# The delta layer's causal convolutions: one pass per tap over a whole channel group in place of three thirds

## The reference

```python
def causal_dwconv(u, buf, w):
    ext = jnp.concatenate([buf.astype(u.dtype), u], axis=1)
    y = ext[:, 0:t] * w[0]
    for j in range(1, CONV_W):           # CONV_W = 4
        y = y + ext[:, j:j + t] * w[j]
    return y, ext[:, t:]

def odd_layer(...):
    u = jnp.dot(hmod, w_in)
    qkv, z, b, a = jnp.split(u, ODD_SPLITS, axis=-1)
    qkv_c, new_buf = causal_dwconv(qkv, conv_buf, conv_w)
    qkv_c = jax.nn.silu(qkv_c).astype(jnp.float32)
    q, k, v = jnp.split(qkv_c, (GDN_KW, 2 * GDN_KW), axis=-1)
    ...                                  # 8 heads of 128: l2_normalize, gated_delta_rule, norm, gate, w_out
```

## Time and profile before

| | |
|---|---|
| time, median of 3 runs | 1657.87 us (1655.21 to 1658.93) |
| the profiled execution's own time | 1660.12 us |
| its span | 1658.3 us |
| PE busy | 1518.7 us, 92% of the span |
| DVE busy | 736.2 us, 44% |
| ACT busy | 410.8 us, 25% |
| POOL busy | 198.1 us, 12% |

### The profile page before, as it was taken

How to read it: one execution, slowest core, us unless ns; L and a number is a source line. 1 busy time by engine, 2 the same in 40 slices (tenths; PEclk the granted TensorE clock), 3 DMA queues, 4 the chain that set the end, 5 groups by cost and what they waited for, 6 DMA issues and landing times.

```text
span 1658.3 us, 32834 instructions
## 1 busy us (share of the span) xinstructions
PE 1518.7 (92%) x14320; PEld 934.1 (56%) x14320; DVE 736.2 (44%) x1650; ACT 410.8 (25%) x1036; POOL 198.1 (12%) x400
## 2 busy tenths in 40 slices
PE   4997999788869997898999999999999999999997
PEld 3554555455544445356766667666676766666533
DVE  4202455333331225264473654736557365562251
ACT  4001343333320004311231312313122131221220
POOL 1000000000001011002030120301213012020020
PEclk8898999999989996898999999999999999999999
DMA  8501111000051304011011110111111111030041
GB/s 336 215 13 44 42 32 62 1 1 1 3 224 58 145 0 170 8 42 42 28 53 31 39 43 29 54 30 39 43 40 43 42 43 27 15 138 3 30 150 64
DMA packets 53012, 100.52 MB, mean 61 GB/s; under 512 B 34458, under 2 KB 37346, under 8 KB 50290
## 3 DMA queue, kind: packets, MB, share of 16 engines
q1 hardware_dynamic: 52868, 98.41, 17.5%
HBM read 83.54 MB, written 14.86 MB: 59 GB/s over the span
## 4 chain that ended last, share of the span: by engine, by line
PE 55%; DVE 4%; issue 2%; ACT 1%; POOL 0%; POOLq 0%; DVEq 0%; ACTq 0%
PE psum L727 53%; PE psum L730 2%; DVE mem L1640 1%; DVE mem L2108 0%; DVE mem L2046 0%; DVE mem L1923 0%; DVE mem L1892 0%; DVE mem L1818 0%; ACT mem L1390 0%; DVE mem L1810 0%; DVE mem L2163 0%; DVE mem L1812 0%; DVE mem L1909 0%; ACT mem L1415 0%; ACT mem L1417 0%
## 5 line engine op out<-in xcount | busy, mean ns | idle before, releaser
L727 PE MATMUL psum<-mem 32*32 32x32 f32 (+9 forms) x13728 | 1441.1, 288 | 74.1 <-issue 23.8
L727 PEld LDWEIGHTS psum<-mem 32*32 32x32 f32 (+5 forms) x13728 | 859.9, 136 | 624.8 <-issue 286.2
L730 PE MATMUL psum<-mem 128*128 128x128 f32 (+1 forms) x592 | 97.1, 303 | 57.2 <-ACT mem L1275 14.2
L1892 DVE SCALAR_TENSOR_TENSOR mem<-mem 128x384 f32<-128x384 f32 (+1 forms) x216 | 138.0, 639 | 2.4
L730 PEld LDWEIGHTS psum<-mem 128*128 128x128 f32 (+1 forms) x592 | 76.7, 160 | 90.2 <-issue 61.9
L1810 DVE SCALAR_TENSOR_TENSOR mem<-psum,mem 128x512 f32<-128x512 f32 x13 | 9.8, 751 | 154.9 <-POOL mem L602 154.9
L1390 ACT ACTIVATE mem<-psum 128x512 f32<-128x512 f32 x26 | 15.3, 593 | 181.4 <-PE psum L727 181.4
L1489 ACT ACTIVATE mem<-psum 128x288 f32<-128x288 f32 (+1 forms) x40 | 15.8, 396 | 175.8 <-PE psum L727 175.8
L1367 ACT ACTIVATE mem<-mem 128x256 f32<-128x256 f32 x72 | 35.5, 496 | 63.7 <-DVE mem L1771 63.7
L1439 ACT ACTIVATE mem<-psum 128x384 f32<-128x384 f32 x48 | 23.4, 490 | 108.2 <-PE psum L727 108.1
L1761 DVE CUSTOM_DVE_ANT_0 mem<-psum,mem 128x256 f32<-128x256 f32 x72 | 25.6, 421 | 50.3 <-PE psum L727 50.3
(11 more groups left out here) (190 smaller groups left out, 986.9 us busy)
## 6 DMA issues: line engine op xcount, KB each, us to landing
mem<-modw SPq DMA_DIRECT2D x12, 2048.0 KB, 9.6
mem<-w SPq DMA_DIRECT2D x44, 512.0 KB, 3.6
x_dram<-mem SPq DMA_DIRECT2D x1, 4608.0 KB, 13.1
mem<-row_dram SPq DMA_DIRECT2D x8, 576.0 KB, 3.6
mem<-x_dram SPq DMA_DIRECT2D x9, 512.0 KB, 3.7
y<-mem SPq DMA_DIRECT2D x9, 512.0 KB, 3.5
mem<-gs SPq DMA_DIRECT2D x8, 512.0 KB, 4.6
ss<-mem SPq DMA_DIRECT2D x8, 512.0 KB, 2.6
```

The source lines that it names most:

```text
L727: return pe.matmul(*a, **k)
L730: return pe.transpose(out, in_, ident[0:n, 0:n])
L1892: x = dve.scalar_tensor_tensor(cvm, U1[:, m, lo + j:hi + j], w, cvm, ALU.mult, ALU.add)
```

## The change

`conv` does nothing for the first two thirds of a channel group. When it is called for the last third it runs the tap over all 1176 columns of the group. The calls, the slots, the order of taps and the semaphores stay as they are; each channel group has four instructions in place of twelve.

```diff
             def conv(h, g, j):
 
                 m, n = divmod(g, 3)
-                lo, hi = n * NC, (n + 1) * NC if n < 2 else UC
+                if n < 2:
+                    return
+                lo, hi = 0, UC
                 w = CW[:, bass.ds(h * 3 + ORDER[m], 1), j]
                 cvm = CV[:, m, lo:hi]
                 if j == 0:
                     dve.wait_ge(sem("pj_ev"), 9 * h + g + 1)
-                    if n == 2:
-                        dve.wait_ge(sem("cs_in"), 48 * h + 48)
+                    dve.wait_ge(sem("cs_in"), 48 * h + 48)
                     c.mark(dve.tensor_scalar(cvm, U1[:, m, lo:hi], w, None, ALU.mult))
                 else:
                     c.sync()
                     x = dve.scalar_tensor_tensor(cvm, U1[:, m, lo + j:hi + j], w, cvm, ALU.mult, ALU.add)
-                    if n == 2 and j == PRE:
+                    if j == PRE:
                         c.tell(x, sem("cv_done"), 3 * h + m + 1)
                     else:
                         c.mark(x)
```

## The result

| | before | changed |
|---|---|---|
| median of 20 runs each | 1658.0 us | 1665.0 us |
| lowest and highest | 1652.7 to 1663.4 us | 1657.2 to 1671.2 us |
| ratio, 95% interval | | 1.0040 [1.0029, 1.0052] |
| span of the profiled execution | 1658.3 us | 1664.2 us |

The change makes the kernel 6.6 us slower by the ratio (4.8 to 8.6 us by its interval; the medians differ by 7.0). The forecast was +7.8 us, 1665.7 us. In the changed file the lines behind the edit carry a number one higher: L1892 is L1893, L2064 is L2065.

The account below looks back on a forecast made before the run. PE, busy for 92% of the span, was taken to bound the kernel, so DVE time counts only where PE waits. Terms -1.8 + 6.6 + 3 = +7.8 us on 1657.87 gave 1665.7 us; range 1658 to 1674.

Parts of the forecast that it names:

- DVE's work: Convolutions on DVE: 192 fewer instructions save 43.8 us, busy time falls from 736 to 692 us, without reaching PE.
- Slot 28: Before the k = 6 residual: its tap goes, ending PE's 0.25 us wait in seven heads; gain 1.8 us.
- The recurrence: Slots 12 to 15 and 23 to 26: longer taps before VN, SP or the residual are hidden; cost 0.
- Rival (a): Recurrence doesn't hide its six longer taps: 0.2 us each in seven heads, 8.4 us more, about 1674 us; chance 0.10.
- Slots 34 to 36: Tail: tap 0's growth hidden; taps 1 and 2 grow 1.60 us against 1.46 us idle before slot 37's gate product.
- Slot 37: Values' last tap, where two heads meet: grows 0.80 us, all on the path PE waits for.
- the left-over: Tail, slots 34 to 36: 0.14 us of tap growth not covered by idle time, added to the stall.
- Rival (b): Tail absorbs its growth, as PE waits for something independent of the tap; about 1656 us; chance 0.10.
- The clock: PE's granted clock behind the stalls where heads meet: a longer stall loses more, +3 us.
- the two spared heads: Two heads whose granted clock stayed at 1.00 behind the stall; taken to lose 1.7 us each after the change.
- the bound: Clock's added loss behind the seven stalls: from 0 to 12 us, the latter if each costs the worst 3.4 us.
- Rival (c): Clock falls behind none of the stalls, so 11.8 us come back: about 1651 us; chance 0.05.

Follow-up runs that it names:

- The second experiment: Against the kernel before: keys and queries in one pass per tap, values' taps as 768 and 408 columns; 0.9983 [0.9964, 1.0002], 1653.5 us.
- the first experiment: Against the kernel before: keys and queries in one pass per tap over 1176 columns, values in thirds as before; 0.9998 [0.9978, 1.0019], 1657.3 us.
- The third experiment: The kernel before with only the values' last tap run whole, over 1176 columns in slot 37; 1.0048 [1.0029, 1.0067], 1664.5 us.
- the fourth: The kernel before with slot 37's tap moved ahead of that slot's gate product; 0.9924 [0.9898, 0.9949], 1644.3 us.

## Why the prediction was right

The measured 1665.0 us and the forecast 1665.7 us differ by less than the runs scatter, so the terms matter more than the sum.

- **DVE's work.** The convolutions' own sum fell by 43.5 us (forecast 43.8), and 43.5 us of work taken off an engine at 44% brought no time. The rule of the Trainium skill (VectorE: DVE Perf Modes, Rules for kernel authors) asks for few operations, and the instructions' cost bears it out (43.5 us for 192); where DVE doesn't bound, it says nothing on the kernel's time. Tap 0 took 829 ns and not 893 ns, in a place that is hidden. The forecast of the engine's busy time, 692 us, was 9 us too low (701.3), because it took sums of durations off a time that counts each moment once. Slot 23 loses a tap too (the queries' second third's last) and not only slots 16 to 22; nothing hangs on it.
- **Slot 28.** The seven waits of 0.25 us are gone. The second experiment isolates them with the tail unchanged and is 2.8 us faster, with an interval from 6.0 us gained to 0.3 us lost. The waits are shown to be gone; that the kernel gains 1.8 us by it is not shown.
- **The recurrence.** Hidden, as forecast. VN and SP lost all their idle time before them and PE did not wait. Rival (a) is out, by the first experiment too.
- **Slots 34 to 36.** Forecast: 0.14 us left over. Measured: none. Tap 1 grew by 0.80 us, but tap 2 by 0.62 only (1.14 to 1.76): it met POOL's masks as before, at a price of 0.33 us where I had carried over 0.5. Their 1.42 us fit into the 1.46 us of idle time, by little. POOL's three masks took 4.02 us and not 2.60; PE's waits name no instruction of POOL.
- **Slot 37.** Forecast 0.80 us, measured 0.81 (stall 3.00 against 2.19), 5.7 us in seven heads instead of the 6.6 with the left-over. The third experiment alone reproduces the change's loss, the fourth takes the stall down by moving this tap. Rival (b), that the tap isn't what PE waits for, is out.
- **The clock.** Forecast +3 us, read as +5.0 us in the one profiled execution. Over all executions the mean clock fell from 0.9616 (of before, beside the experiments) to 0.9573, which is about 7 us of the span (5 to 10 by the scatter), again an upper value. (The execution of the earlier trace rows had a mean of 0.958, low for that kernel.) So the direction is shown and the term was too small. I had taken the two spared heads to lose 1.7 us each; in the trace the loss grew by 1.7, 3.4 and 1.7 us in three heads and fell by 1.7 in one. The 3.4 us that I took for the worst came from the two heads with the second gap, which I hadn't seen; the changed kernel loses as much in two heads that have none (near 976 and 1184 us), so the bound stands. Rival (c) had the direction wrong: no kernel whose stall was longer than that of before lost less than before.

The terms as measured, -1.8 + 5.7 + 5.0, make 8.9 us, and the spans differ by 5.9. Of the missing 3 us, 1.6 lie behind the last stall, where the changed kernel's execution took 173.9 us and that of before 175.5, and 1.2 between the first and the last restart of PE, where it took 7.3 us more and the terms make 8.5; why is open. The forecast's closeness is thus partly luck: a clock term that was too small, a left-over that didn't come, and these 3 us, which no term of the prediction foresaw. What the runs confirm is the path, slot 37's tap, and its 0.80 us a head.

## What to carry to other kernels

Merging short instructions took 43.5 us off an engine that doesn't bound this kernel, and brought no time. The merged instruction is later and longer, and what counts is where its last piece stands: ask which of the pieces lay on the path (here one of a head's twelve merged taps), and leave that one short. Look also at what an in-order engine waits for right before the critical piece; here the piece could go into that wait, which gained nearly twice what the change lost (12.6 against 6.6 us). Merge where there is cover and split at the end: 768 columns early and 408 late had fewer instructions and not the longer stall, though by itself its time can't be told from that of before.

## What the runs showed that I had not expected

The clock's loss falls with the stall in steps that I hadn't thought of: in the five heads without the second gap nothing at 0.91 us, up to 5.2 us at 2.19 and 2.41, and about twice that at 3.0, with no more at 3.8. Shortening a stall by 1.28 us in seven heads, 9 us, gave 12.6 us.

The second gap in two of the seven heads stands in every kernel of this study, whatever form the convolutions have. Its cause was not tried, and neither was what ends the stall of 0.91 us. As the clock falls behind it even where the stall is short (3.4 us in two heads), it would be the next thing to look at.

The tap of DVE that meets POOL's masks did not pay more for being longer: 0.5 us more on 408 columns (1.14 us against 0.63), 0.33 us more on 1176 (1.76 us against 1.43).
